# Modulation chunks moved into the rounds of the first two MLPs, and all low parts of the query, key and value weights on VectorE

## The reference, cut to what matters

```python
cond = jax.nn.silu(c)
for i in range(2):
    mod = cond @ ada_w[i] + ada_b[i]                 # 1024 x 6144
    sh1, sc1, g1, sh2, sc2, g2 = split(mod, 6)
    h = rms_norm(x, mix_norm_g[i]) * (1.0 + sc1) + sh1
    y = conformer_conv(h, ...) if i == 0 else moba_attention(h, w_qkv, ..., w_o)
    x = x + g1 * y
    h = rms_norm(x, mlp_norm_g[i]) * (1.0 + sc2) + sh2
    x = x + g2 * (square(relu(h @ mlp_w1[i])) @ mlp_w2[i])
```

## Time and profile before

| | us |
|---|---|
| median of 3 runs | 1109.22 (1107.02 to 1109.81) |
| the profiled execution | 1110.23 |
| its span, first to last instruction | 1108.4 |
| TensorE busy in it | 1053.7 |
| VectorE busy | 709.8 |
| ScalarE busy | 491.9 |
| GpSimd busy | 133.4 |

### The profile page before, as it was taken

One profiled execution on the slowest core, in us unless ns is written; L12 is line 12 of the kernel. 1 busy time (PEld: TensorE's weight loads), 2 busy tenths in 40 slices (PEclk: granted clock), 3 DMA queues, 4 the chain that ended last, 5 costly groups with the idle time before them and its releaser, 6 DMA issues.

```text
span 1108.4 us, 16827 instructions
## 1 busy us (share of the span) xinstructions
PE 1053.7 (95%) x6872; PEld 928.2 (84%) x6872; DVE 709.8 (64%) x831; ACT 491.9 (44%) x554; POOL 133.4 (12%) x74
## 2 busy tenths in 40 slices
PE   6999998999999999998999999998978799999998
PEld 6997776899999989976799999986856489989996
DVE  4868556687667687433696777668784748454463
ACT  5345536444344445432544433445324835444441
POOL 0030002010010040022011000001132501100000
PEclk9999999999999999999999999999889999999999
DMA  8884335738787753657258877863664324656540
GB/s 287 301 303 141 125 114 173 269 113 313 265 289 270 271 163 118 181 146 245 76 188 307 271 259 269 300 228 114 229 230 150 114 77 137 197 170 200 187 172 38
DMA packets 119740, 221.58 MB, mean 200 GB/s; under 512 B 6338, under 2 KB 20740, under 8 KB 119684
## 3 DMA queue, kind: packets, MB, share of 16 engines
q1 hardware_dynamic: 119056, 219.17, 58.5%
q0 software_dynamic: 432, 1.57, 0.5%
q10 hardware_dynamic: 196, 0.05, 0.0%
HBM read 215.07 MB, written 1.05 MB: 195 GB/s over the span
## 4 chain that ended last, share of the span: by engine, by line
PE 80%; DVE 10%; ACT 5%; issue 3%; DMA 1%; SPq 1%; ACTq 0%; POOL 0%; DVEq 0%
PE ps L417 75%; DVE ada_acc L869 2%; ACT hi L347 2%; PE ps L855 2%; PE ps L454 1%; PE ps L731 1%; DVE lo L358 1%; PE ps L657 1%; DMA raw<-in_w_in 0%; DVE hTl L504 0%; ACT aS L1592 0%; DVE stat L1890 0%; ACT gate L1491 0%; DMA prow<-in_c 0%; DVE aS L1885 0%
## 5 line engine op out<-in xcount | busy, mean ns | idle before, releaser
L358 DVE TENSOR_TENSOR lo<-raw,hi 128x2048 fp32r<-128x2048 f32 x147 | 345.7, 2357 | 273.2 <-ACT hi L347 272.7
L347 ACT ACTIVATE hi<-raw 128x2048 fp32r<-128x2048 f32 x153 | 292.4, 1913 | 348.7 <-PE ps L417 335.1
L417 PE MATMUL ps<-hTh,hi 128*128 128x256 f32 x992 | 282.7, 285 | 2.0 <-DVE hTl L504 1.9
L417 PE MATMUL ps<-hTh,lo 128*128 128x256 f32 x992 | 280.7, 283 | 0.0
L417 PE MATMUL ps<-hTl,hi 128*128 128x256 f32 x992 | 280.7, 283 | 0.0
L417 PEld LDWEIGHTS ps<-hTh,hi 128*128 128x128 f32 x992 | 190.3, 192 | 3.8 <-DVE hTl L504 2.5
L417 PEld LDWEIGHTS ps<-hTl,hi 128*128 128x128 f32 x992 | 190.3, 192 | 0.3
L417 PEld LDWEIGHTS ps<-hTh,lo 128*128 128x128 f32 x992 | 190.3, 192 | 0.0
L417 PE MATMUL ps<-hi,hidh 128*128 128x512 f32 x416 | 162.8, 391 | 0.4 <-DVEq L652 0.4
L417 PE MATMUL ps<-hi,hidl 128*128 128x512 f32 x416 | 162.1, 390 | 0.0
L417 PE MATMUL ps<-lo,hidh 128*128 128x512 f32 x416 | 162.0, 389 | 0.0
(11 more groups left out here) (216 smaller groups left out, 909.3 us busy)
## 6 DMA issues: line engine op xcount, KB each, us to landing
raw<-in_mlp_w SPq DMA_DIRECT2D x64, 1024.0 KB, 5.3
ada_raw<-in_ada_w SPq DMA_DIRECT2D x48, 1024.0 KB, 7.3
raw<-in_w_in SPq DMA_DIRECT2D x21, 1024.0 KB, 7.3
raw<-in_w_ff_in SPq DMA_DIRECT2D x16, 1024.0 KB, 5.4
raw<-in_w_ff_out SPq DMA_DIRECT2D x16, 1024.0 KB, 6.8
raw<-in_attn_w_qkv SPq DMA_DIRECT2D x12, 1024.0 KB, 6.3
raw<-in_conv_w_in SPq DMA_DIRECT2D x8, 1024.0 KB, 5.6
taps<-u_pad SPq DMA_DIRECT2D x64, 71.0 KB, 2.8
```

What stands on the lines that cost most here:

```text
L347: nc.scalar.activation(hi[:, slot], raw[:, slot], ACT.Copy).then_inc(hi_made, 1)
L358: nc.vector.tensor_tensor(lo[:, slot], raw[:, slot], hi[:, slot].bitcast(F32), ALU.subtract).then_inc(lo_made, 1)
L417: return nc.tensor.matmul(o, lhs, rhs, start=start, stop=False, skip_group_check=True)
```

## The change

Three chunks are worked on in each round of the first two MLPs in place of two, with an accumulator each (`ada_acc` becomes a list of three). The head and tail chunks get new numbers. No chunk is left in the input stage or in the stage of queries, keys and values, and 24 are worked on as before. A fourth number in a chunk's tuple names its accumulator. Three tables give the places in a round: `ADA_STEPS` (at which j VectorE takes which half of which chunk), `ADA_LOADS` (behind which j SP loads it) and `ADA_KEEPS` (at which j a chunk is kept). TensorE sums after j = 3, j = 5 and j = 7. In the stage of queries, keys and values VectorE makes all twelve low parts.

```diff
-        ada_acc = acc_area("ada_acc", 0, [P, 512])
+        ada_acc = [acc_area("ada_acc0", 0, [P, 512])]
...
+        ada_acc += [big("ada_acc1", 12288, [P, 512]), big("ada_acc2", 14336, [P, 512])]
...
-            pe.wait_ge(ada_kept, (10, 18, 18, 24)[2 * layer + i] + 1)
+            pe.wait_ge(ada_kept, (11, 22, 22, 24)[2 * layer + i] + 1)
...
+            def loop_sum(q, i):
+                if m < 2:
+                    ada_sum(pe, ada_loop(m, i)[q])
...
-                if m < 2:
-                    ada_sum(pe, ada_loop(m, i)[0][0])
+                loop_sum(0, i)
                 first(2, n + 4, s + 4, 2 * i + (8 * m + 2))
+                loop_sum(1, i)
                 second(1, n + 6, s + 6, 2 * i + (8 * m + 2))
-                if m < 2:
-                    ada_sum(pe, ada_loop(m, i)[1][0])
+                loop_sum(2, i)
...
-        ADA_IN = [(0, 0, 6), (1, 0, 7)]
-        ADA_QKV = [(18 + q, 1, 6 + q) for q in range(4)]
-
-        ADA_HEAD = ((2, 0, 8), (10, 0, 10), (22, 1, 10))
-        ADA_TAIL = ((9, 0, 9), (17, 0, 11), (23, 1, 11))
+        ADA_HEAD = ((0, 0, 0, 2), (11, 0, 11, 2), (22, 1, 10, 2))
+        ADA_TAIL = ((10, 0, 10, 0), (21, 1, 9, 0), (23, 1, 11, 0))
+
+        ADA_STEPS = {0: (0, 0), 2: (0, 1), 3: (1, 0), 4: (1, 1), 5: (2, 0), 6: (2, 1)}
+        ADA_LOADS = {1: (0, 0), 2: (0, 1), 4: (1, 0), 6: (1, 1), 7: (2, 0), 8: (2, 1)}
+        ADA_KEEPS = {4: 0, 6: 1, 7: 2}
 
         def ada_loop(m, i):
 
-            return [(2 * i + (8 * m + 3 + q), m, 2 * i + q) for q in range(2)]
+            return [(3 * i + (11 * m + 1 + q), m, 3 * i + (1 - m + q), q) for q in range(3)]
...
+            number, acc = chunk[0], ada_acc[chunk[3]]
             pe.wait_ge(ada_step, number * 8 + 16)
             pe.wait_ge(ada_kept, number + 1)
             for q in range(4):
-                last = nc.tensor.matmul(ps[:, 6, q:q + 1], ada_acc[:, q * P:(q + 1) * P],
+                last = nc.tensor.matmul(ps[:, 6, q:q + 1], acc[:, q * P:(q + 1) * P],
...
-                    if ada is not None and j % 2 == 0:
-                        ada_unit(dve, ada[j // 4][0], j // 2 % 2)
+                    if ada is not None and j in ADA_STEPS:
+                        q, h = ADA_STEPS[j]
+                        ada_unit(dve, ada[q], h)
                     dve_step(dve, u + j, j=s + j)
                     if j % 4 == 1:
                         lo_of(1 - j // 4, chunk + j // 4)
-                    if ada is not None and j in (3, 7):
-                        ada_keep(dve, ada[j // 7])
+                    if ada is not None and j in ADA_KEEPS:
+                        ada_keep(dve, ada[ADA_KEEPS[j]])
...
-                for j in range(8):
-                    c = 2 * i + (2, 1, 3, 2)[j // 2]
-                    (first, second)[j // 2 % 2](n + j, s + j, c, j % 2)
-                    if m < 2 and j % 2 == 0:
-                        ada_load(sp, ada_loop(m, i)[j // 4], j // 2 % 2)
+                for j in range(9):
+                    if j < 8:
+                        c = 2 * i + (2, 1, 3, 2)[j // 2]
+                        (first, second)[j // 2 % 2](n + j, s + j, c, j % 2)
+                    if m < 2 and j in ADA_LOADS:
+                        q, h = ADA_LOADS[j]
+                        ada_load(sp, ada_loop(m, i)[q], h)
...
-                    elif 2 * c + h >= 5:
-                        half = 2 * c + h - 5
-                        ada_load(sp, ADA_IN[half // 2], half % 2)
             load(sp, U_GV, win[:, :, 2048:2304])
-            ada_load(sp, ADA_IN[1], 1)
...
-                    if 2 <= c:
-                        ada_load(sp, ADA_QKV[c - 2], h)
...
-                if h == 0:
-                    ada_sum(pe, 0)
...
-            ada_sum(pe, 1)
...
-                ada_sum(pe, ADA_QKV[0][0])
-                pe.wait_ge(ada_kept, 18 + 2)
                 gate_row(pe, 1, 0)
 
             qkv(0)
             qkv(1, first_unit_done)
             pe.wait_ge(row_kept, 3)
-            qkv(2, lambda: ada_sum(pe, ADA_QKV[1][0]))
-            qkv(3, lambda: ada_sum(pe, ADA_QKV[2][0]))
-            qkv(4, lambda: ada_sum(pe, ADA_QKV[3][0]))
-            pe.wait_ge(ada_kept, 22 + 1)
+            qkv(2)
+            qkv(3)
+            qkv(4)
...
-            act.wait_ge(ada_step, 8 + 8 * 2)
...
-                if u in (2, 3, 5, 6):
-                    ada_unit(dve, *((0, 0), (0, 1), (), (1, 0), (1, 1))[u - 2])
...
-                if 1 <= c < 5:
-                    ada_keep(dve, ADA_QKV[c - 1])
-                dve_step(dve, U_QKV + 2 * c, turn=c > 0)
-                if c < 4:
-                    for h in range(2):
-                        ada_unit(dve, ADA_QKV[c][0], h)
+                for h in range(2):
+                    dve_step(dve, U_QKV + 2 * c + h)
...
-            pool.wait_ge(ada_kept, 2 + 1)
...
-            for c in range(6):
-                pool_step(pool, U_QKV + 2 * c + 1)
```

More of the change, by code:

```diff
@@ L754, in mlp_pe @@
                                  skip_group_check=True)
-            ada_sum(pe, ADA_HEAD[m][0])
+            ada_sum(pe, ADA_HEAD[m])
             def first(c, u, j, chunk):
@@ L782, in mlp_pe @@
             second(0, n + 2, n + 2, 8 * m + 7,
-                   (lambda: ada_sum(pe, ADA_TAIL[m][0]), (lambda: gate_row(pe, m - 1, 1)) if m else None))
+                   (lambda: ada_sum(pe, ADA_TAIL[m]), (lambda: gate_row(pe, m - 1, 1)) if m else None))
             second(1, n + 4, n + 4, 8 * m + 8, final=True)
@@ L828, in mlp_pool @@
                 square(c + 8 * m, True)
-        ADA_IN = [(0, 0, 6), (1, 0, 7)]
-        ADA_QKV = [(18 + q, 1, 6 + q) for q in range(4)]
-        ADA_HEAD = ((2, 0, 8), (10, 0, 10), (22, 1, 10))
-        ADA_TAIL = ((9, 0, 9), (17, 0, 11), (23, 1, 11))
+        ADA_HEAD = ((0, 0, 0, 2), (11, 0, 11, 2), (22, 1, 10, 2))
[3 more added lines that the diff above has]
+        ADA_KEEPS = {4: 0, 6: 1, 7: 2}
         def ada_loop(m, i):
-            return [(2 * i + (8 * m + 3 + q), m, 2 * i + q) for q in range(2)]
+            return [(3 * i + (11 * m + 1 + q), m, 3 * i + (1 - m + q), q) for q in range(3)]
         def ada_load(sp, chunk, h):
-            number, layer, c = chunk
+            number, layer, c, _ = chunk
             sp.wait_ge(ada_step, number * 8 + (4 * h + 4))
@@ L848, in ada_load, with ada_sum @@
             sp.dma_start(ada_raw[:, h], src).then_inc(ada_landed[h], 16)
-        def ada_sum(pe, number):
+        def ada_sum(pe, chunk):
+            number, acc = chunk[0], ada_acc[chunk[3]]
             pe.wait_ge(ada_step, number * 8 + 16)
@@ L854, in ada_sum, with ada_unit @@
             for q in range(4):
-                last = nc.tensor.matmul(ps[:, 6, q:q + 1], ada_acc[:, q * P:(q + 1) * P],
+                last = nc.tensor.matmul(ps[:, 6, q:q + 1], acc[:, q * P:(q + 1) * P],
                                         ones[:, 0:1], start=True, stop=True)
             last.then_inc(ada_cols, 1)
-        def ada_unit(dve, number, h):
+        def ada_unit(dve, chunk, h):
+            number, acc = chunk[0], ada_acc[chunk[3]]
             dve.wait_ge(ada_landed[h], number * 16 + 16)
@@ L865, in ada_unit @@
                 if h == 0 and k == 0:
-                    ins = nc.vector.tensor_scalar(ada_acc[:], w, s, None, ALU.mult)
+                    ins = nc.vector.tensor_scalar(acc[:], w, s, None, ALU.mult)
                 else:
                     dve.wait_ge(ada_step, step)
-                    ins = nc.vector.scalar_tensor_tensor(out=ada_acc[:], in0=w, scalar=s, in1=ada_acc[:],
+                    ins = nc.vector.scalar_tensor_tensor(out=acc[:], in0=w, scalar=s, in1=acc[:],
                                                          op0=ALU.mult, op1=ALU.add)
@@ L876, in late_steps @@
                 if chunk is not None:
-                    ada_unit(dve, chunk[0], h)
+                    ada_unit(dve, chunk, h)
                 dve_step(dve, last - 1 + h)
         def ada_keep(dve, chunk):
-            number, layer, c = chunk
+            number, layer, c, _ = chunk
             dve.wait_ge(ada_cols, number + 1)
@@ L914, in mlp_dve @@
                 if j < 2:
-                    ada_unit(dve, ADA_TAIL[m][0], j)
+                    ada_unit(dve, ADA_TAIL[m], j)
                 dve_step(dve, u0 + 26 + j)
@@ L1635, in _ @@
                                             ALU.mult).then_inc(par_ok, 1)
-                if u == 4:
-                    ada_keep(dve, ADA_IN[0])
                 if u == 3:
@@ L1641, in _ @@
                                           pair(2).rearrange("p b n -> p (b n)")).then_inc(kT_kept, 1)
-            ada_keep(dve, ADA_IN[1])
             def gelu(i, x, dst):
```

## The result

The changed kernel takes 1116.65 us (median of 4 runs, 1115.06 to 1117.84), and the kernel before, run beside it, 1108.86 us. The ratio is 1.0071, with an interval of 1.0059 to 1.0083: it is slower by 0.7%, 7.8 us by the medians. The profiled execution took 1115.48 us with a span of 1113.7, and time and span are each 5.3 us more than those of the profiled execution before.

A forecast was written before the change was run, and what follows sets the result against it. TensorE, busy 1053.7 of 1108.4 us, was taken as the bound. Queries, keys and values -22.0, input stage -1.1 and rounds +26.5 gave +3.4 us, from the median 1109.22 to 1112.6, rounded to 1113; range 1101 to 1123.

The forecast's parts named there:

- The sum: Whole kernel: all terms together +3.4 us, from the median 1112.6, rounded to 1113 us; slower given 0.46.
- Queries, keys and values, -22.0: That stage, without its chunks: TensorE's gaps, four sums and low clock go, 62.1 us becoming 40.1.
- Input stage, -1.1: Input stage: two TensorE sums go, gaining 1.1 us within 0.5 to 2.1, the rest lost to a longer wait.
- First wait: MLP round: TensorE's second sum waits 1.6 us for the first chunk to be kept, 2.5 in first rounds.
- VectorE's wait for the half: MLP round: VectorE waits 3.0 us for the second chunk's second half, landing 7.2 us after its issue.
- The replay of VectorE's queue: First MLP's second round, stepped through instruction by instruction: 50.75 us, where it took 46.64.
- Second wait: MLP round: TensorE's third sum waits 1.5 us for the second chunk to be kept.
- the rival with the clock, 1131: MLP rounds: gaps bring TensorE's clock down in every round, six times 3 us added; chance 0.10.
- the six rounds: Rounds of the first two MLPs: 26.5 us longer together, 4.7 of it the six more sums.
- GpSimd's square: MLP round: GpSimd's 1.90 us square and VectorE's first half of the third chunk hold each other up.
- the rival in which GpSimd costs nothing, 1104 us: MLP rounds: first wait there, second gone, six rounds 9 us shorter; chance 0.13.
- No loss in the rounds, 1091: Rival: MLP rounds take the third chunk without loss, only the sums count, 1090.8 us; chance 0.10.

The follow-up runs named there:

- e8_qkv_bare: Kernel before, without the four chunks among queries, keys and values (worked on nowhere) and with all twelve low parts by VectorE: 1089.45 us, ratio 0.9814.
- e10_fill2_short: Changed kernel with 8 extra matmuls on constants on TensorE ahead of the second sum of each round: 1117.66 us, ratio 1.0074.
- e2_keeps: Changed kernel with the first chunk kept behind j = 3 and the second behind j = 5, loads unchanged: 1101.41 us, ratio 0.9947.
- e7_act_square: e2_keeps with the squares of all three MLPs by ScalarE instead of GpSimd: 1094.86 us, ratio 0.9869.
- e1_both: Changed kernel with the first two chunks kept earlier and the second chunk's second half and both third-chunk halves loaded earlier: 1090.83 us, ratio 0.9836.
- e3_loads: Changed kernel with only the load of the second chunk's second half moved one place earlier: 1120.82 us, ratio 1.0126.
- e4_keep0: Changed kernel with only the first chunk kept earlier, behind j = 3: 1126.39 us, ratio 1.0153.
- e9_qkv_pool: Changed kernel with GpSimd again making every second low part among queries, keys and values: 1117.24 us, ratio 1.0068.

## Why the prediction was right, and where its steps were not

**The sum.** Forecast 1113 us, range 1101 to 1123, slower the likeliest; measured 1116.65. From span to span the forecast was +3.4 us and the trace has +5.3. The medians are 7.8 apart, because before's profiled execution lay 1.4 us above the median of the kernel before, 1108.86, and after's 1.2 below its own. The longer executions of the changed kernel (spans of 1116.0) show a granted clock of 0.981 on average, the shorter ones (1113.3 to 1113.7) 0.983, and 0.002 of 1056 busy us are about the 2 us between them; where they lose it wasn't looked for. That the sum comes this near is in part luck: in the rounds a cost that was priced at nothing (the low clock, 1.65 us) stands in the place of one that was priced at 1.5 and isn't there.

**Queries, keys and values, -22.0:** the trace has -23.0 to the transposes, of which 0.67 are the gap ahead of them that I expected back, and +0.6 from there on: -22.4. In e8_qkv_bare 2.4 came back, so the error of 1 us that I allowed for the stage was too small, since it left out where the clock falls in attention. The profiled execution was a good one in this: e10_fill2_short, with the same code there, gains only 20.9 (143.1 for 164.0 from norm to norm).

**Input stage, -1.1:** -1.9, within its bounds of 0.5 to 2.1. I had taken a value near the lower bound, since the wait of 1.18 us at 87.86 was to grow by most of what was gained. It is gone from the trace after; in its place TensorE is idle for 1.96 us at 72.53, where it had no gap before. So the term is nearly right in size and wrong in its path.

**First wait, 1.6 us, and 2.5 in the first rounds:** 1.7 to 1.9 us, and in the first rounds 3.3 (first MLP) and 2.5 (second). The 3.3 could have been seen: in the kernel before, the half issued at 269.6, in the first round of the first MLP, took 8.5 us to land, and I had taken the second MLP's 8.1 for both; after the change the two land in 8.7 and 7.8. VectorE's wait for the half, forecast as 3.0, is 3.22, the landing 7.28. The replay of VectorE's queue was good to 0.2 us: first chunk kept 36.7 us into the round (forecast 36.6), second 49.7 (49.9).

**Second wait, 1.5 us:** it isn't there. This is the step that failed in its mechanism: I gave the clock a chance of 0.10 and set its threshold by the length of a gap, "between 1.73 and 3.65", from the earlier trace rows. In the rounds it fell behind every gap, the one of 1.72 included, while the gap of 1.73 in the stage of attention had full clock behind it. The fall costs some 1.65 us on the next two units (12.64 for 10.93 to 11.04) and takes the place of the second wait, so a round has 51.3 us where I had 50.75. e10_fill2_short shows it: where the clock doesn't fall, the second wait appears, 0.9 us and not 1.5, and a round takes 50.6 to 50.8 us, the forecast's own figure. For the same reason the rival with the clock, 1131, was wrong in its price: it took 3 us for a fall and added them to a wait that hides the fall in part. What is not hidden, and the longer first waits, are the 3.3 us that the six rounds missed (29.8 for 26.5).

**GpSimd's square:** it met the chunk instruction as foreseen (1.98 us for 0.48), 1.5 us more, where the replay had 1.7 and the rival without it 1.9. In the changed kernel the low clock covers it; in e2_keeps, without such a cover, it costs TensorE about 1 us a round (e7_act_square). So the rival in which GpSimd costs nothing, 1104 us, was wrong about VectorE, and right that TensorE doesn't wait a second time, for another reason.

**No loss in the rounds, 1091:** this rival's time is what the tables of e1_both give, 1090.8.

## What to carry to other kernels

When work is put into a full loop, replay the queue of the engine that does it, position by position, and ask for each result not when it is ready but behind what it is handed over: here the chunks' sums were done, and the keeping of one, a copy of 0.15 us, stood one place too late, behind a transfer. Two waits in one round hide each other: cure one alone and the other grows (e3_loads, e4_keep0 were slower than no cure), cure both and 26 us come back. And a gap on TensorE in a dense loop has to be priced with the low clock behind it, but only as far as no later wait covers it.

## What was not expected of the hardware

- In a dense loop TensorE's clock fell to 0.50 behind gaps of 1.7 to 3.3 us, and in the changed kernel the price didn't grow with the gap: some 1.65 us each. But a fall hasn't one price: behind gaps of 2.56 us e3_loads lost 1.5 us or 3.0, and behind gaps of 2.9 to 3.1 us e4_keep0 lost 1.5 us three times and 2.6 to 3.1 three times. The costly one of e3_loads (windows):

```profile
294.00:298.00 4.00, 4.00 (x21) 4.00 (x22) 3.93 (x5) 0.00 (x0) 0.00 (x0) 0.56 0.97 301
298.00:302.00 4.00, 4.00 (x23) 4.00 (x23) 1.02 (x2) 0.00 (x0) 0.00 (x0) 0.58 1.05 395
```

- The length of a gap alone doesn't tell whether the clock falls. Most gaps of 0.7 to 1.1 us in e2_keeps had 1.00 behind them, but one of 0.97 was followed by a fall, and so was one of 0.90 in e10_fill2_short. One of 1.73 between transposes had 1.00 in the kernel before. The gap of 2.62 us ahead of the second group of transposes had 1.00 behind it in the changed kernel (844.6 to 849.6) and 0.66 in e9_qkv_pool (845.6 to 850.6).
- In the second MLP the fall came late: 1.00 for more than a microsecond after the sum that ended the gap, and only then 0.50 (windows of the changed kernel; the sum starts at 673.18 and takes 1.05 us).

```profile
674.20:675.30 1.10, 1.10 (x6) 0.91 (x6) 1.06 (x2) 0.58 (x2) 0.61 (x1) 1.00 1.04 406
675.70:678.60 2.90, 2.90 (x8) 2.28 (x7) 2.83 (x4) 0.20 (x1) 0.00 (x0) 0.50 0.87 328
```
